# First Strassen chunk and last layer norm of a two-block transformer kernel: two waits moved on TensorE, the last norm reordered

## The reference

```python
def layer_norm(x, g, b):
    x32 = x.astype(jnp.float32)
    mu = jnp.mean(x32, axis=-1, keepdims=True)
    var = jnp.mean(jnp.square(x32 - mu), axis=-1, keepdims=True)
    y = (x32 - mu) * lax.rsqrt(var + LN_EPS)
    return (y * g.astype(jnp.float32) + b.astype(jnp.float32)).astype(x.dtype)

def swiglu_2(h, w_in, w_out):
    gate, up = jnp.split(h @ w_in, 2, axis=-1)
    return (jax.nn.silu(gate) * up) @ w_out
# second block, last sublayer of each layer
    y = swiglu_2(modulate(x, mod, 2), ffn_w_in[l, 1], ffn_w_out[l, 1])
    x = layer_norm(DN_ALPHA * x + 0.5 * sub_gate(mod, 2) * y, ln_g[l, 2], ln_b[l, 2])
```

## Time and profile before

| what | value |
|---|---|
| median of 3 runs | 2124.78 us |
| their range | 2124.2 to 2128.8 us |
| the profiled execution's own time | 2124.72 us |
| its span, first to last instruction | 2122.9 us |
| TensorE busy | 2084.2 us, 98% of the span |
| VectorE, ScalarE, GpSimd busy | 1272.6, 422.6, 495.0 us |
| mean granted TensorE clock | 0.991 |
| chain that ended last | TensorE 88%, VectorE 7%, DMA 2% |

### The profile page before, as it was taken

The page is one execution under the profiler, slowest core; times in us unless marked ns, Lnnn a source line. Parts: engine busy times, 40 slices in busy tenths (PEclk is TensorE's granted clock), DMA queues, the critical chain, the costliest instruction groups (busy, mean ns, idle before and its releaser), DMA issues.

```text
span 2122.9 us, 24027 instructions
## 1 busy us (share of the span) xinstructions
PE 2084.2 (98%) x9428; PEld 1675.1 (79%) x9428; DVE 1272.6 (60%) x2509; ACT 422.6 (20%) x804; POOL 495.0 (23%) x411
## 2 busy tenths in 40 slices
PE   7999999999999999999999999999999999999997
PEld 4777888688876887687788888688868868888865
DVE  5546588746776466746523687777776653346554
ACT  3334211022110111033130311031102323122101
POOL 0100244402543244300000144414440000002340
PEclk9999999999999999999999999999999999999998
DMA  9673576775768564842334475766574333444431
GB/s 376 248 268 98 201 285 244 275 264 204 298 241 297 200 245 188 293 166 103 155 124 154 160 281 236 273 235 242 227 256 174 131 154 119 159 158 159 153 134 70
DMA packets 61551, 437.85 MB, mean 206 GB/s; under 512 B 6976, under 2 KB 8768, under 8 KB 40448
## 3 DMA queue, kind: packets, MB, share of 16 engines
q1 hardware_dynamic: 28608, 317.82, 38.8%
q0 software_dynamic: 32256, 117.45, 15.8%
q10 hardware_dynamic: 576, 1.05, 0.1%
HBM read 434.20 MB, written 2.10 MB: 206 GB/s over the span
## 4 chain that ended last, share of the span: by engine, by line
PE 88%; DVE 7%; DMA 2%; POOL 1%; issue 1%; ACT 1%; SPq 1%; ACTq 0%; DVEq 0%; POOLq 0%
PE lin L1881 27%; PE small_ps L2027 18%; PE lin L2027 13%; PE small_ps L2089 5%; PE lin L2122 5%; PE lin L2089 4%; PE small_ps L1881 3%; PE lin L2353 3%; PE pstat L2004 1%; PE lin L2278 1%; DVE proj L1131 1%; DVE ada_ring L1095 1%; PE small_ps L2372 1%; DMA ada_ring<-in_ada 1%; DMA rec<-in_ada_pe 1%
## 5 line engine op out<-in xcount | busy, mean ns | idle before, releaser
L1881 PE MATMUL lin<-h,ring 128*128 128x256 f32 x1968 | 434.2, 382 | 4.4 <-ACT h L1000 2.4
L1881 PEld LDWEIGHTS lin<-h,ring 128*128 128x128 f32 x1968 | 373.9, 191 | 60.1 <-issue 8.8
L630 POOL TENSOR_TENSOR proj<-ring 128x1024 f32<-128x1024 f32 x54 | 127.8, 2366 | 836.6 <-DVE xc L1310 633.4
L1095 DVE CUSTOM_DVE_ANT_0 ada_ring<-ada_ring,crow 128x1024 f32<-128x1024 f32 x224 | 265.9, 1220 | 32.9 <-DMA ada_ring<-in_ada 32.5
L615 POOL DMA_DIRECT2D ada_ring<-in_ada x224 | 121.4, 542 | 702.3 <-DVE sums L1095 667.8
L2027 PE MATMUL small_ps<-ring,h 128*128 128x256 f32 x864 | 195.6, 379 | 4.8 <-DVE sq L1112 4.8
L2027 PEld LDWEIGHTS small_ps<-ring,h 128*128 128x128 f32 x864 | 163.8, 190 | 28.4 <-issue 6.2
L2027 PE MATMUL lin<-proj,sq 128*128 128x256 f32 x672 | 153.9, 379 | 0.0
L2027 PEld LDWEIGHTS lin<-proj,sq 128*128 128x128 f32 x672 | 127.7, 190 | 17.4
L1881 PE MATMUL lin<-rec,ring 128*128 128x258 f32 (+2 forms) x608 | 139.5, 380 | 0.0
L1881 PEld LDWEIGHTS lin<-rec,ring 128*128 128x128 f32 x608 | 115.2, 190 | 16.8
(11 more groups left out here) (428 smaller groups left out, 3038.0 us busy)
## 6 DMA issues: line engine op xcount, KB each, us to landing
ring<-in_w SPq DMA_DIRECT2D x66, 2048.0 KB, 8.9
ada_ring<-in_ada POOLq DMA_DIRECT2D x224, 512.0 KB, 5.9
ring<-in_w2a SPq DMA_DIRECT2D x30, 1536.0 KB, 7.7
ring<-in_gates SPq DMA_DIRECT2D x12, 2048.0 KB, 8.0
ring<-in_w2d SPq DMA_DIRECT2D x12, 1408.0 KB, 7.3
ring<-in_mproj SPq DMA_DIRECT2D x8, 2048.0 KB, 7.9
ring<-in_mtok SPq DMA_DIRECT2D x4, 2048.0 KB, 8.2
ring<-in_branch SPq DMA_DIRECT2D x4, 2048.0 KB, 7.6
```

The source lines that it names most:

```text
L630: W(combined_weights(j, 0), b12, b11, ALU.subtract).then_inc(s_weights_combined, 1)
L1095: V.tensor_tensor_reduce(w, w, crow[:, 0 if s < FIRST2 else 1], 1.0, 0.0, ALU.mult, ALU.add, sums[:, s % 3, b:b + 1]).then_inc(s_ada_used, 1)
L1881: ins = mm(dst, w[:, lo:lo + m], rhs(k), start=k == 0, stop=k == nk - 1)
```

## The change

Two edits.

1. First chunk of every feed-forward, on TensorE: the wait for the four sums of `h` moves from before product 1 to before product 3. And before product 5 a folded sublayer waits for the fourth raw unit's results to be scaled (`raw_scaled`), which empties the bank, and no longer for the silu and gate times up that follow.
2. The last layer norm. A multiplication in the middle of the eighth unit sums the seven tiles that are done. While TensorE finishes the unit, VectorE centres these seven by their own mean and ScalarE squares them, VectorE adds up both. The eighth tile is centred by the same mean and added. The true mean (of what was centred) and the sum of the squares come from two multiplications; the variance is the mean square less the square of that mean; the centred tiles are corrected by the mean. ScalarE does a root of one column ahead of the last square, which loads its table of functions early. VectorE gives the last two tiles their gain and shift, ScalarE the first six.

```diff
             for k in range(0, KD, 2):
-                sp.wait_ge(s_x_new, k + 2)
+                if k < FINAL_BY_ACT:
+                    sp.wait_ge(s_x_new, k + 2)
+                else:
+                    sp.wait_ge(s_final_tiles, KD - FINAL_BY_ACT)
                 sp.dma_start(out[:, k:k + 2], x[:, k:k + 2]).then_inc(s_result_dma, 16)
...
-            fold_in(len(subs), None)
-            for k in range(KD):
+            for k in range(0, KD - 2, 2):
+                act.wait_ge(s_x_centred, nth(act, s_x_centred))
+                A(sq[:, k:k + 2], xc[:, k:k + 2], ACT.Square).then_inc(s_fold_squares, 1)
+            act.wait_ge(s_x_centred, nth(act, s_x_centred))
+            A(sq[:, KD - 2], xc[:, KD - 2], ACT.Square).then_inc(s_fold_squares, 1)
+            A(lbv[:, 0, 0:1], eps[:, 1:2], ACT.Sqrt)
+            act.wait_ge(s_x_centred, nth(act, s_x_centred))
+            A(sq[:, KD - 1], xc[:, KD - 1], ACT.Square).then_inc(s_fold_squares, 1)
+            act.wait_ge(s_final_mean_taken, 1)
+            A(sq[:, 2], sq[:, 3], ACT.Square).then_inc(s_final_square, 1)
+            act.wait_ge(s_final_variance, 1)
+            A(sd[:], sq[:, 4], ACT.Sqrt, bias=eps[:, 1:2]).then_inc(s_deviation, 1)
+            for k in range(FINAL_BY_ACT):
                 g, b = VC["ln_g"] + 8 * (len(subs) - 1 - FIRST2) + k, VC["ln_b"] + 8 * (len(subs) - 1 - FIRST2) + k
                 act.wait_ge(s_x_scaled, nth(act, s_x_scaled))
                 A(x[:, k], xc[:, k], ACT.Identity, scale=vec[:, g:g + 1], bias=vec[:, b:b + 1]).then_inc(s_x_new, 1)
...
+            most = (KD - 1) * P
+            final_sum, final_squares = yab[:, 0], yab[:, 1]
+
+            def final_first_tiles():
+
+                dve.wait_ge(s_mean_sums, nth(dve, s_mean_sums))
+                for k in range(0, KD - 2, 2):
+                    V.scalar_tensor_tensor(xc[:, k:k + 2], pa[2][:, 0:T].unsqueeze(1).broadcast_to([P, 2, T]), -1.0 / most,
+                                           x[:, k:k + 2], ALU.mult, ALU.add).then_inc(s_x_centred, 1)
+                V.scalar_tensor_tensor(xc[:, KD - 2], pa[2][:, 0:T], -1.0 / most, x[:, KD - 2],
+                                       ALU.mult, ALU.add).then_inc(s_x_centred, 1)
+                V.scalar_tensor_tensor(final_sum, pa[2][:, 0:T], -1.0 / P, rstd[:], ALU.mult, ALU.add).then_inc(s_dve_chain, 1)
+                nth(dve, s_x_centred, 4)
+                dve.wait_ge(s_fold_squares, nth(dve, s_fold_squares, 4))
+                for n, (a, b) in enumerate(((sq[:, 0:2], sq[:, 2:4]), (sq[:, 0:2], sq[:, 4:6]), (sq[:, 0], sq[:, 1]))):
+                    V.tensor_tensor(a, a, b, ALU.add).then_inc(s_dve_chain, 1)
+                    dve.wait_ge(s_dve_chain, nth(dve, s_dve_chain, 1 if n else 2))
+                V.tensor_tensor(final_squares, sq[:, 0], sq[:, KD - 2], ALU.add).then_inc(s_dve_chain, 1)
+                dve.wait_ge(s_dve_chain, nth(dve, s_dve_chain))
+
+            def final_last_tile(u):
+
+                dve.wait_ge(*taken(u))
+                V.scalar_tensor_tensor(xc[:, KD - 1], pa[2][:, 0:T], -1.0 / most, x[:, KD - 1],
+                                       ALU.mult, ALU.add).then_inc(s_x_centred, 1)
+                dve.wait_ge(s_x_centred, nth(dve, s_x_centred))
+                V.tensor_tensor(final_sum, final_sum, xc[:, KD - 1], ALU.add).then_inc(s_final_parts, 1)
+                dve.wait_ge(s_fold_squares, nth(dve, s_fold_squares))
+                V.tensor_tensor(final_squares, final_squares, sq[:, KD - 1], ALU.add).then_inc(s_final_parts, 1)
+
+            def final_norm():
+
+                mean = sq[:, 3].unsqueeze(1).broadcast_to([P, 2, T])
+                dve.wait_ge(s_final_mean, 1)
+                V.tensor_scalar(sq[:, 3], pstat[:, 0:T], -1.0 / D, None, ALU.mult).then_inc(s_final_mean_taken, 1)
+                dve.wait_ge(s_final_mean_taken, 1)
+                for k in range(0, KD, 2):
+                    V.tensor_tensor(xc[:, k:k + 2], xc[:, k:k + 2], mean, ALU.add).then_inc(s_x_centred, 1)
+                    if k == 0:
+                        dve.wait_ge(s_final_square, 1)
+                        dve.wait_ge(s_final_squares, 1)
+                        V.scalar_tensor_tensor(sq[:, 4], pa[3][:, 0:T], 1.0 / D, sq[:, 2],
+                                               ALU.mult, ALU.subtract).then_inc(s_final_variance, 1)
+                dve.wait_ge(s_x_centred, nth(dve, s_x_centred, 4))
+                make_rstd(rstd[:])
+                for k in range(KD):
+                    V.tensor_tensor(xc[:, k], xc[:, k], rstd[:], ALU.mult).then_inc(s_x_scaled, 1)
+                dve.wait_ge(s_x_scaled, tiles_scaled(len(subs)) + KD)
+                for k in range(FINAL_BY_ACT, KD):
+                    g, b = VC["ln_g"] + 8 * (len(subs) - 1 - FIRST2) + k, VC["ln_b"] + 8 * (len(subs) - 1 - FIRST2) + k
+                    V.tensor_scalar(x[:, k], xc[:, k], vec[:, g:g + 1], vec[:, b:b + 1], ALU.mult, ALU.add).then_inc(s_final_tiles, 1)
...
-                    if s >= FIRST2 and m:
+                    if s + 1 == len(subs) and m == KD - 1:
+                        final_last_tile(u0 + m)
+                    elif s >= FIRST2 and m:
                         dve.wait_ge(*taken(u0 + m))
                         before = x[:, 0] if m == 1 else rstd[:]
                         V.tensor_tensor(rstd[:], before, x[:, m], ALU.add).then_inc(s_tiles_added, 1)
                         dve.wait_ge(s_tiles_added, nth(dve, s_tiles_added))
                     if name == "wf":
                         ada(ADA_IN_WF[m])
+                    if s + 1 == len(subs) and m == KD - 2:
+                        final_first_tiles()
...
-            fold_statistics(len(subs))
-            scaled_tiles(len(subs))
+            final_norm()
...
                 h_tile(KD - 1)
-                pe.wait_ge(s_h_combined, 4 * (f + 1))
                 for j in range(CHUNKS):
                     n = ph.first + RAW // 2 + j
                     slot_of(ph, 0, RAW // 2 + j)
@@ -2042,9 +2122,13 @@
                     part(2, quarter_of_h(1, 0), b21).then_inc(s_second_product, 1)
                     if j:
                         turn_hidden(s, j - 1)
+                    else:
+                        pe.wait_ge(s_h_combined, 4 * (f + 1))
                     part(3, combined_h(3), b22)
                     if j:
                         pe.wait_ge(s_second_gate, before + j)
+                    elif folded(s):
+                        pe.wait_ge(s_raw_scaled, RAW * raw_before(s) + RAW)
                     else:
                         pe.wait_ge(*taken(u0 + RAW - 1))
...
                     for k in range(KF):
                         if m == 6 and k in (8, 14, 20):
                             turn_results((k - 8) // 6)
+                        if s + 1 == len(subs) and m == KD - 1 and k == KF // 2:
+                            pe.wait_ge(s_tiles_added, nth(pe, s_tiles_added, KD - 2))
+                            mm(pa[2][:, 0:T], ones[:], rstd[:], start=True, stop=True).then_inc(s_mean_sums, 1)
                         ins = mm(lin[(u + m) % NBANK][:, 0:T], w[:, k * P:(k + 1) * P], big[:, k], start=k == 0, stop=k == KF - 1)
                     ins.then_inc(s_unit, 1)
...
-            mean_summed()
-            folded_squares_summed()
+            for n, done in enumerate((s_final_mean, s_final_squares)):
+                pe.wait_ge(s_final_parts, n + 1)
+                mm((pstat, pa[3])[n][:, 0:T], ones[:], yab[:, n], start=True, stop=True).then_inc(done, 1)
```

More of the change, by code:

```diff
@@ L72 @@
 CHUNKS = KF // 2 - RAW // 2
+FINAL_BY_ACT = 6
 PAIRS = [2, 2, 2, 2, 2, 1]
@@ L291, in build @@
         s_base_made = sem("residual_base_made")
+        s_final_parts = sem("final_parts")
+        s_final_mean = sem("final_mean")
+        s_final_mean_taken = sem("final_mean_taken")
+        s_final_square = sem("final_square_of_mean")
+        s_final_squares = sem("final_squares")
+        s_final_variance = sem("final_variance")
+        s_final_tiles = sem("final_tiles")
         s_even_kept = sem("even_parts_kept")
@@ L419, in spectral, with raw_before @@
             return s < len(subs) and subs[s] == "fourier"
+        def raw_before(s):
+            return sum(folded(n) for n in range(s))
         def folds_before(s):
```

## The result

| | median | runs | range |
|---|---|---|---|
| kernel before | 2126.86 us | 14 | 2123.15 to 2131.99 |
| changed kernel | 2130.55 us | 14 | 2126.68 to 2136.67 |

The ratio is 1.0019 with an interval of 1.0010 to 1.0028: the change costs 3.7 us where 5.4 were to be gained. The prediction held that less than 4.25 us can't be told from nothing; with 14 runs of each kernel it can, as the interval lies clear of 1. The profiled execution took 2130.59 us (span 2128.8), 5.9 more than that of before.

The account below looks back on a forecast made before the run. TensorE, busy 98% of the span, was taken as the bound. From 2124.72 us, 2.04 for the first chunks (0 + 0.84 + 1.20) and 3.4 for the last norm gave 2119.3 us, range 2117.3 to 2121.8.

Parts of the forecast that it names:

- the one at s = 6: First chunk at s = 6: product 5 starts 1.20 us earlier, but the second chunk starts as before, so 0 gained.
- was not the later one: At s = 6, product 6 ended at 1221.47; GpSimd's subtraction L630 was taken to follow the last DMA issue instead.
- s = 7: First chunk at s = 7: following the course of s = 6, 0.84 of a 1.29 us lead is kept.
- s = 9: First chunk at s = 9: no `ada` there, nothing catches VectorE, and the whole 1.20 us is kept.
- All three chunks keep their gain: Rival on the first chunks: 3.69 us gained there plus 3.4 at the end, giving 2117.6 us; chance 0.11.
- an `ada` a little earlier would free it: Argument for all chunks keeping their gain: VectorE's addition L1144 is caught by only some tenths; earlier `ada` avoids that.
- The first edit gives nothing: Rival: L1144 or a later addition is caught at s = 7 and 9, or other waits take the gain; 2121.3 us, chance 0.09.
- Slower: the clock: Rival: pauses halve TensorE's clock in all three first chunks, costing 9.6 us, giving 2128.9 us; chance 0.03.
- The last norm: End of the program: overlapping seven tiles with TensorE's last unit moves the end by 3.4 us.
- The rival by which the end gives half: End of the program: the last norm gains only 1.85 us, giving 2120.8 us; chance 0.15.
- its three mishaps: At the end: one sum at half clock, stores costing 0.5 us more, first tiles 0.5 later; 1.85 us gain left.
- the "wrong" ones: Signs against the forecast: L630 before its DMA issue allows, eighth tile waiting over 1 us, first-chunk clock below 1.00.

Follow-up runs that it names:

- chunks_only: Kernel before with both first-chunk waits moved and the last norm as it was: 2132.89 us, ratio 1.0030 to the kernel before.
- issue_after: Changed kernel with GpSimd's last DMA issue moved behind its subtractions for the second chunk: 2128.07 us, ratio 1.0005 to the kernel before.
- seventh_wait: Changed kernel, GpSimd's first subtraction for the second chunk also waiting for the seventh product: 2117.52 us, ratio 0.9960 to the kernel before; repeated, 2118.90 us, 0.9959.
- norm_only: Changed kernel with the first edit undone, so only the last norm is new: 2123.60 us, ratio 0.9982 to the kernel before.
- before_held: Kernel before, GpSimd's first subtraction for the second chunk also waiting for VectorE's four additions: 2126.01 us, ratio 0.9998 to the kernel before.
- first_wait_only: Kernel before with only the wait for the sums of `h` moved to product 3: 2130.93 us, ratio 1.0016 to the kernel before.

## Why the prediction was wrong

**The step that failed** is the one at s = 6: "None of this hangs on TensorE's being early, so the second chunk still starts at 1225.05". The recorded start of GpSimd's subtraction indeed did not move: 0.93 us behind VectorE's first addition in both traces. I took the start as all that matters. But in the kernel before, product 6 came in 0.1 us after the last DMA issue had begun, which I read as "was not the later one", as if ties cost nothing; a lead of 1.4 us puts it clearly ahead, and then the third addition is caught, and behind two subtractions instead of one. The term was 0; it is a loss of 5.0 us.

**s = 7** used s = 6 of the kernel before as its template and fell with it: a gain of 0.84 became a loss of 3.3. Its own sum put product 6 only 0.04 us behind the start of the last DMA issue (1435.85 and 1435.81), where it could be on either side. The template held for the DMA issue (L645 follows it as forecast), not for what VectorE then waits for. **s = 9** was right in kind, nothing is caught, and its forecast was too small: 1.4 us measured, 1.20 forecast. The lag behind L1337 that I took from L1112 as 0.36 was 0.06, 1217.34 to 1217.40 at s = 6. Together the first edit was to give 2.04 us and costs 6.9 by the trace, 6.3 by chunks_only.

**The rule** of the Trainium skill, "SBUF — State Buffer", section "Who interferes with whom", was the right one to weigh: an instruction with two SBUF inputs on VectorE and one of GpSimd that reads SBUF exclude each other, and the later waits for the whole of the earlier. issue_after agrees (2.56 us behind a subtraction of 2.50 that had begun 0.22 earlier). What I drew from it was too little. By the rule as I used it only one subtraction is ever waited for; 5.19 us behind two, by an addition recorded first, is not in it, and there the measurement decides. My price for a collision came from the one at this place, 2.45 us, though GpSimd has two such instructions in a row and the same trace has holds of 3.93 and 3.94 us elsewhere, through both.

**The rivals.** "All three chunks keep their gain" was named, with "an `ada` a little earlier would free it"; seventh_wait and its repeat gain 8.5 and 8.7 us by their ratios against its 7.1, once GpSimd is kept off. "The first edit gives nothing", because L1144 or another addition is caught at s = 7 too, had the mechanism but not its size. "Slower: the clock" gave 2128.9, the nearest number, for another reason: it let the clock fall behind pauses of 0.4 to 1.3 us. The pauses before product 5 left it at 1.00. It fell at two of three places, behind 4.11 and 2.98 us of idleness that only the collision made, and cost 2.3 and 1.6 us there by the shifts. The rival was thus priced without the wait that leads to it, and got 3 in 100; its nearness to the measured time is luck.

**The last norm** was right: 3.4 us forecast, 3.5 by the trace, 3.0 by the medians of norm_only. 14.7 us were forecast from the unit's end to the end of the span, 14.69 measured. Its steps hold: VectorE late by 0.5 (0.6 forecast), TensorE's sum 0.67 at full clock, the reciprocal 1.75, ScalarE's six tiles 3.06 (3.05). From the last store's issue, 2126.53, to the end it is 2.3 us, 2.2 forecast. The rival by which the end gives half has fallen with that, though one of its three mishaps did come up: in norm_only's trace the first sum ran at half clock (1.19 us and not 0.67), and the end gave 3.0 there.

**Of the signs** named in advance two of the "wrong" ones were of use: the granted clock did fall in a first chunk, but GpSimd did *not* start earlier than its DMA issue allows. The sign that would have told was the length of the additions, which I had listed for s = 7 only.

## What to carry to other kernels

Before an engine is given a lead, list what its counts release, and for each instruction so released ask what it excludes, for the whole of the run of such instructions and not for the one that the old trace shows at that place. Look through the whole old trace for the longest hold of the kind: here it was there, 3.93 us, where it cost nothing. When an instruction has two possible releasers that come within some tenths of each other, its start alone doesn't tell what a lead will do; put its release behind the work that it could hold (here one wait on GpSimd, which turned a loss of 3.7 us into a gain of more than 8). A harmless collision in the old trace, as the 2.45 us here that cost next to nothing (before_held), is a place where slack is being used up.

## What was not expected of the hardware

- A VectorE addition of two SBUF operands, 0.42 us alone, was held 5.19 us behind two GpSimd subtractions back to back, though its record begins 0.25 us before the first of them, while a DMA issue still ran on GpSimd. With the second subtraction kept back it was 2.90; where GpSimd's count came later, nothing or one subtraction's length. In the kernel before, an addition of 128 x 8, 0.17 us alone, was held 3.93 us in the same way.
- VectorE's instructions with an operand in PSUM (L1234, L1229) ran at 0.41 to 0.43 us all along beside GpSimd's subtraction in seventh_wait.
- TensorE's clock went to 0.50 behind 2.98 us of idleness (changed kernel, s = 7: 16 records in 5.38 us) and stayed at full behind 2.93 (first_wait_only, s = 6: 3.69 us). At s = 8 it also fell with TensorE busy all through, in the 128 x 8 products or right behind them, in both traces: a single execution can be some us off for that alone. In two other traces it didn't fall there.
